# Toeplitz panels of the S5 layer staged in DRAM beside the projections, and loaded as one transfer each

## The reference, cut to what matters

```
for rev in (0, 1):
    abar, bbar, cmat = s5_discretise(lam_re[rev], lam_im[rev], log_step[rev], ...)
    yc_dir, h_ctx = s5_scan(flip_seq(uc, rev), abar, bbar, cmat, h0)
    y_dir, _ = s5_scan(flip_seq(u, rev), abar, bbar, cmat, h_ctx)
    y = y + flip_seq(y_dir, rev)
glu(y): g = gelu(y); g * sigmoid(g @ w + bias)
```

## Time and profile before

| what | value |
|---|---|
| median of 3 runs | 2614.7 us (2610.75 to 2618.63) |
| the profiled execution | 2603.0 us, span 2601.2 us |
| granted TensorE clock, mean | 0.915 |
| PE busy | 2217.0 us (85%) |
| DVE / ACT / POOL busy | 52% / 35% / 19% |
| chain that ended last | PE 60%, DVE 14%, POOL 10%, DMA 5%, ACT 5%, issue 4% |
| DMA | 324.38 MB, mean 125 GB/s |

### The profile page before, as it was taken

How to read it: one execution, slowest core, us unless ns; L and a number is a source line. 1 busy time by engine, 2 the same in 40 slices (tenths; PEclk the granted TensorE clock), 3 DMA queues, 4 the chain that set the end, 5 groups by cost and what they waited for, 6 DMA issues and landing times.

```text
span 2601.2 us, 33804 instructions
## 1 busy us (share of the span) xinstructions
PE 2217.0 (85%) x13593; PEld 1674.9 (64%) x13593; DVE 1362.3 (52%) x2527; ACT 908.3 (35%) x1779; POOL 505.1 (19%) x457
## 2 busy tenths in 40 slices
PE   6878788769899867479988988779999987877998
PEld 5757667547557566379754444558888855546998
DVE  4548677544346999355443356443333233455554
ACT  3224454442222442144322244332222222344443
POOL 0047878402047970000000011000000000000000
PEclk8989999889999988689988988889999998998999
DMA  8254454633443228976552211333322342315553
GB/s 280 74 172 129 135 148 125 202 112 108 146 99 89 77 75 161 257 217 168 160 156 65 81 66 49 105 105 98 97 87 79 110 114 65 110 53 162 179 170 106
DMA packets 423666, 324.38 MB, mean 125 GB/s; under 512 B 65086, under 2 KB 411470, under 8 KB 422358
## 3 DMA queue, kind: packets, MB, share of 16 engines
q1 hardware_dynamic: 386452, 295.70, 39.0%
q10 hardware_dynamic: 34242, 16.92, 2.3%
q0 software_dynamic: 2816, 9.60, 1.1%
HBM read 292.42 MB, written 29.75 MB: 124 GB/s over the span
## 4 chain that ended last, share of the span: by engine, by line
PE 60%; DVE 14%; POOL 10%; DMA 5%; ACT 5%; issue 4%; SPq 1%; ACTq 1%; DVEq 0%; POOLq 0%
PE ps L119 58%; POOL A L88 9%; DVE A L88 3%; ACT A L115 3%; PE ps L122 2%; DMA wbuf<-ctab 2%; DVE R L88 2%; DVE A L102 2%; DVE A L92 2%; DVE A L105 2%; DVE A L93 1%; SPq L125 1%; DVE A L96 1%; POOL A L125 1%; DMA wbuf<-in_ada_w 1%
## 5 line engine op out<-in xcount | busy, mean ns | idle before, releaser
L119 PE MATMUL ps<-R,R 128*128 128x256 f32 (+1 forms) x3968 | 844.2, 335 | 33.5 <-ACT R L115 23.4
L119 PEld LDWEIGHTS ps<-R,R 128*128 128x128 f32 x3968 | 631.8, 194 | 114.9 <-ACT R L115 28.6
L119 PE MATMUL ps<-HR,R 128*128 128x512 f32 (+1 forms) x1984 | 565.3, 370 | 35.2 <-DVE R L88 24.8
L88 DVE TENSOR_TENSOR R<-wbuf,R 128x1024 fp32r<-128x1024 f32 (+2 forms) x304 | 332.9, 1104 | 368.1 <-ACT R L115 368.0
L119 PEld LDWEIGHTS ps<-HR,R 128*128 128x128 f32 x1984 | 355.8, 193 | 101.3 <-issue 34.1
L115 ACT ACTIVATE A<-ps 128x512 f32<-128x512 f32 (+4 forms) x400 | 210.3, 556 | 587.8 <-PE ps L119 411.1
L88 POOL TENSOR_TENSOR A<-A 128x512 f32<-128x512 f32 (+3 forms) x258 | 295.8, 1161 | 526.4 <-DVE A L96 270.2
L88 DVE TENSOR_TENSOR A<-A 128x128 f32<-128x128 f32 (+4 forms) x796 | 359.4, 481 | 63.0 <-ACT A L115 26.2
L115 ACT ACTIVATE R<-wbuf 128x1024 fp32r<-128x1024 f32 (+2 forms) x304 | 270.1, 894 | 290.9 <-PE ps L119 264.7
L119 PE MATMUL ps<-H,wbuf 128*128 128x512 f32 (+2 forms) x928 | 342.2, 527 | 13.6 <-DVE H L93 13.5
L119 PE MATMUL ps<-A 128*128 128x64 f32 (+10 forms) x1736 | 293.4, 366 | 27.7 <-DMA wbuf<-ctab 9.0
(11 more groups left out here) (102 smaller groups left out, 1622.3 us busy)
## 6 DMA issues: line engine op xcount, KB each, us to landing
wbuf<-in_w_ada SPq DMA_DIRECT2D x48, 1024.0 KB, 5.2
wbuf<-in_ada_w SPq DMA_DIRECT2D x24, 1024.0 KB, 10.3
wbuf<-in_w_out SPq DMA_DIRECT2D x24, 1024.0 KB, 5.6
wbuf<-in_w_ffn_gate SPq DMA_DIRECT2D x22, 1024.0 KB, 5.3
wbuf<-in_w_ffn_up SPq DMA_DIRECT2D x22, 1024.0 KB, 5.9
wbuf<-in_w_ffn_down SPq DMA_DIRECT2D x32, 704.0 KB, 4.6
wbuf<-in_attn_w_in SPq DMA_DIRECT2D x20, 1024.0 KB, 6.9
ctab<-A ACTq DMA_DIRECT2D x64, 256.0 KB, 2.8
```

Of the source, the lines that this page charges most:

```text
L88: return self.op(lambda e: e.tensor_tensor(out, a, b, op))
L119: return self.op(lambda e: e.matmul(out, lhsT, rhs, start=start, stop=stop, skip_group_check=True))
```

## The change

It adds a DRAM tensor `ttab` of 8 Toeplitz panels, already in the form in which they are used. During the projections, for b = 2 to 5, SyncE issues for each half of b one panel's eight copies of 128 KB from `kf` to `ttab` (64 copies in all). `panels_sp` waits for the last of them in place of the wait for `kf`, and loads each Toeplitz panel from `ttab` as one transfer of 1 MB to all 128 partitions, in rows of 8 KB. The modulation pieces stay where they are.

```diff
+        self.ttab = dram("ttab", 8, 128, 2048)
...
+        self.l_tt = sig("landed_toeplitz")
...
+    def toeplitz_sp(self, sp, a):
+
+        if a == 0:
+            sp.wait_ge(self.l_kf, 15)
+        src = self.kf.rearrange("(a g) n f -> a n g f", a=8)[a]
+        for t in range(8):
+            sp.dma(self.ttab[a, 16 * t:16 * t + 16].rearrange("p (g f) -> p g f", g=16),
+                   src[:, :, 16 * (7 - t):16 * (7 - t) + 128]).then_inc(self.l_tt, a)
...
     def panels_sp(self, sp, q):
         if q == 0:
-            sp.wait_ge(self.l_kf, 15)
+            sp.wait_ge(self.l_tt, 7)
             sp.wait_ge(self.l_ct[0], 30)
             sp.wait_ge(self.l_ct[1], 31)
...
             else:
-                src = self.kf.rearrange("(a g) n f -> a n g f", a=8)[2 * q + i]
-                for t in range(8):
-                    sp.dma(s[16 * t:16 * t + 16].rearrange("p (g f) -> p g f", g=16),
-                           src[:, :, 16 * (7 - t):16 * (7 - t) + 128]).then_inc(sem, key)
+                sp.dma(s, self.ttab[2 * q + i]).then_inc(sem, key)
...
                     halves(u, lambda: step(projs[b]))
                     u += 2
+                    if b < 6:
+                        part("toeplitz", u // 2 - 1)
```

More of the change, by code:

```diff
@@ L1610, in flow @@
                ("enter", "act"): self.enter_act, ("enter", "dve"): self.enter_dve, ("recur", "dve"): self.recur_dve,
-               ("before", "act"): self.before_act, ("before", "dve"): self.before_dve, ("panels", "sp"): self.panels_sp,
+               ("before", "act"): self.before_act, ("before", "dve"): self.before_dve, ("panels", "sp"): self.panels_sp, ("toeplitz", "sp"): self.toeplitz_sp,
                ("leave", "pe"): self.leave_pe, ("leave", "act"): self.leave_act, ("leave", "dve"): self.leave_dve}
```

## The result

The changed kernel takes 2593.5 us in the median of four runs (2588.5 to 2596.3), beside 2616.5 us for the kernel before; the ratio is 0.9913, 95% interval [0.9889, 0.9937]. Run again later beside other kernels, it came to 0.9898 [0.9881, 0.9914]. I had forecast 2598.7 us, 0.6% less than before; it is 0.9 to 1.0% less. The first median lies inside the range of 2590 to 2611 us, the later one, 2588.1 us, just under it. The median of the kernel before moved between 2612.3 and 2616.5 us from one such comparison to the next, so the ratios, each taken beside its own runs of the kernel before, say more than microseconds across comparisons.

What follows compares the result with a forecast made beforehand. The prediction took PE's waits for `ctab` panels behind slow Toeplitz bytes as the bound. A stage gain of 16 us and copies at 0 gave 2614.7 - 16 = 2598.7 us, range 2590 to 2611.

Steps and rivals of the forecast that it cites:

- The bound: Panel stage: PE waits 38.0 us in ten pieces for `ctab` panels, which stand behind slow Toeplitz bytes in SyncE's queue.
- The Toeplitz load: Panel stage: a 1 MB Toeplitz panel in one transfer takes 2.7 us, the `ctab` rate, instead of 9.0 us.
- The steps on PE: Panel stage from y(0,0) to y(3,1): block ends followed one by one, y(3,1) at 1097.9 instead of 1115.7 us.
- The three blocks of 10.4 us each: y(0,1), y(1,0), y(1,1): each takes 5.65 us to land plus 4.7 us of matmuls; gain 6.5 us by y(1,1).
- The mis-sized term: Gain of the panel stage: 17.8 us, less 1.8 for six landings with more queued around them, net 16 us.
- The copies: During the projections, on SyncE's queue: 18 us per b, hidden by the lead before units 16 to 21; cost 0.
- a sign of being wrong: End of z, before the panel stage: z ending later than 1011.7 us would speak against the forecast.
- the rival of a held-up shipping: Projections: copies at D = 36 to 38 us delay shipping, PE stands about 59 us more; 2658 us, chance 0.08.
- The rival of slow landings: Panel stage: `ctab` panels still land in 8.2 us, a block costs 12.9; gain 4.4, 2610.3 us, chance 0.14.
- PE gets everything in time: Panel stage from y(2,0) on falls toward its own PE and ACT steps, some 6 us lower; 2592 us, chance 0.10.
- The last rival: Panel stage: t panels load no faster, as if 512-byte runs were not the reason; no change, 2614.7 us, chance 0.04.
- The whole time: Whole kernel: 16 us less from the panel stage, copies at 0, so a median of 2598.7 us.

Runs made afterwards that it cites:

- e1_copies_only: Against the changed kernel: the 64 copies are still issued, but panels load from `kf` in eight transfers as before; 2613.8 us, ratio 1.0002 to the kernel before.
- e5b_copies_thrice: Against the changed kernel: each copy made three times, two into tensors nobody reads; 2616.9 us, ratio 1.0023 to the kernel before.

## Why the prediction was right

**The bound** was named rightly: DMA bytes ahead of the `ctab` panels, most of them Toeplitz. The kernels without copies, with short runs and with six slots each show a side of it.

**The Toeplitz load**, taken at 2.7 us, ran at 397 GB/s alone and, among `ctab` panels, at 395, which is 2.7 us for 1 MB. I had left open whether the form or the run of the transfer makes the rate; it is the form, one transfer over all partitions, which gives 310 to 329 GB/s even with runs of 512 bytes.

**The steps on PE**, relative to y(0,0)'s start and with the forecast ahead: y(1,1) ended at 36.0 and at 35.5 us; y(2,0) began at 51 and at 48.4; y(2,1) ended at 61 and at 59.8; y(3,1) at 80.0 and at 77.5. The three blocks of 10.4 us each were right to half a microsecond, so the 0.3 us that I had added for each of six landings with other bytes around them, 1.8 us in all, were not needed. After y(2,0) two small misses cancel: y(2,1) ended 11.4 us after y(2,0)'s start where I had 10, and the two blocks after it took 17.6 us where I had 18.9. The rest of the difference lies before y(2,0). The modulation panel let PE start 5.3 us after its issue (1056.5 to 1061.81) where I had kept the 6.1 us from y(1,1)'s end of before, and its matmuls took 1.36 us instead of 1.94. And I had charged 5.8 us from the start of ScalarE's copies to y(2,0); it was 1069.32 - 1064.46 = 4.9. The row of before gives that wait to ScalarE; since the same copies release PE sooner here, I read it now as the landing of c0 behind the Toeplitz bytes. Other profiles support this: in nine of them, with old and new loads, ScalarE releases y(2,0) after a wait of 5.20 to 5.24 us, and in e1_copies_only, with the loads of before, the same wait is 7.67 us and put down to the `ctab` panel. For the profile before itself it stays argued and not shown. **The mis-sized term** is thus the gain of the stage, 17.8 less 1.8 = 16 in the prediction, 20.2 in the trace. Part of it is the clock, which I had not counted: the same matmuls took 6.3 us less.

**The copies**, taken at 18 us per round and at a cost of 0, took 10.4 us, and that is SyncE's issue time, 16 times 0.65 us. The engines moved them at 343 to 345 GB/s once several were queued, faster than the stores of `ctab` at 280. The Trainium skill (DMA: Bandwidth & Descriptors, Latency and other measured facts) has 207 to 214 GB/s for its DRAM to DRAM copies; here the measurement is higher and decides. The last load back from `scr` for b = 5 was issued by 851.7 us, 0.6 us sooner than before once the later start of 3.0 us is taken off. The end of z at 1014.65 us instead of 1011.7, a sign of being wrong in the prediction, is that same later start: from the beginning of the projections to y(0,0) both profiles take 299.7 us. So the rival of a held-up shipping fell by its price, and its mechanism was confirmed by the copies made three times.

**The rival of slow landings** fell: from the release to PE's start it takes 5.1 to 6.1 us. The median landing of `ctab` panels, 8.2 us before, is 6.5 us now, so part of it was the bytes ahead.

**The other two rivals.** That PE gets everything in time is not what happened, although its 2592 us lies nearer the measured 2593.5 than my own 2598.7: from y(2,0) to the end the stage took 29.1 us, my steps gave 28.9, and the waits of 2.56 and 5.32 us are still there. The last rival expected no gain if the runs of 512 bytes were not the reason for the slow rate. They were not the main one, and the load was fast all the same, because the change widened the transfer too.

**The whole time.** I forecast -16 us. The two comparisons give -23 and -27 us by their ratios, the stage -20. The 3 to 7 us more I can't place for certain. Every kernel that was timed here gained more by its ratio than its profiled stage shows (for e5b_copies_thrice, whose time goes elsewhere, this can't be told): the changed kernel 3 and 6 us in its two comparisons, the six slots 1.5, the copies alone 2, the short runs 2, the two halves 2 and 5, the loads alone 4, the six slots without the change 7, the two kernels with eight transfers 10 and 11. What they share is the one profile of the kernel before, an execution some 12 us under the median. Its stage of 97.7 us may have been a short one, as the 100.2 us of e1_copies_only suggest, and that would be some 2 us of each; this is argued and not shown, since the kernel before was profiled once. The rest stays open. So the range was hit although the gain of 23 to 27 us was underrated by 7 to 11.

## What to carry to other kernels

Ask of every DMA how many partitions its destination spans before counting its run length: a tile written in eight strips of 16 neighbouring partitions cost 9.0 us per MB here in runs of 512 bytes and some 8 in rows of 8 KB, in one transfer of 128 partitions 2.7. If a tile can only be built in strips, build it in DRAM where a queue has a lead, measure that lead (here the time between the shipped data's landing and its first use), and load it whole. And look for the next bound at once: the extra slots were worth nothing before the change and 9 to 13 us after it.

## What the runs showed of the hardware

The granted clock of TensorE gave nearly a third of the stage's gain, 6.3 of 20.2 us (5.3 of 20.5 with the second profile of the changed kernel). It is 0.65 in the mean before and 0.75 after over the same matmuls; a group of 48 takes 2.79 us at the lower of the two levels (1.2 GHz) and 1.52 at the higher (2.4 GHz), as the rows at 1093.49 and 1096.85 show. I had counted every block at one length.

The same clock moves the rest of the kernel from one execution to the next. From the end of y(3,1) to the last matmul the profiled executions took between 1480 and 1492 us, over 7596 matmuls in all and a program that is the same there. The kernel before, and the changed one:

```profile
1115.70:2597.30 1481.60, 1325.64 (x7596) 1002.04 (x7596) 668.58 (x1044) 513.83 (x940) 37.45 (x72) 0.93 0.37 111
```

```profile
1098.40:2590.60 1492.20, 1335.96 (x7596) 1009.32 (x7596) 668.78 (x1044) 513.84 (x940) 37.37 (x72) 0.92 0.36 111
```

PE is idle for the same 156 us in both. The whole difference of 10.6 us is in the busy time of the same matmuls, 1336.0 instead of 1325.6 us, at a mean granted clock of 0.92 instead of 0.93. What chooses between the two was not tried.
